# 96 token slots per expert and pass instead of 128 in a float32 mixture-of-experts kernel on one core

## The reference

```python
D_MODEL = 1024; SEQ = 256; D_FF = 3584; N_EXPERTS = 8; TOP_K = 2

def moe_ffn(h, router, w_gate_up, w_down):
    t = h.reshape(B * S, D)
    logits = (t @ router).astype(jnp.float32)
    top_v, top_i = lax.top_k(logits, TOP_K)
    gates = jax.nn.softmax(top_v, axis=-1)
    combine = jnp.sum(jax.nn.one_hot(top_i, N_EXPERTS) * gates[..., None], axis=1)
    out = jnp.zeros_like(t)
    for e in range(N_EXPERTS):
        out = out + combine[:, e:e + 1] * swiglu(t, w_gate_up[e], w_down[e])
    return out.reshape(B, S, D)

def swiglu(h, w_gate_up, w_down):
    g, u = jnp.split(h @ w_gate_up, 2, axis=-1)
    return (jax.nn.silu(g) * u) @ w_down
```

## Time and profile before

| what | value |
|---|---|
| median of 3 runs | 1673.5 us (1673.34 to 1674.12) |
| the profiled execution | 1673.83 us |
| its span, first to last instruction | 1672.0 us |
| mean granted TensorE clock | 0.968 |
| busy: PE, PEld, DVE, ACT | 94%, 74%, 66%, 54% |
| expert layer | from about 632 us to the end |
| HBM | 430 MB, 257 GB/s over the span |

### The profile page before, as it was taken

The page is one execution under the profiler, slowest core; times in us unless marked ns, Lnnn a source line. Parts: engine busy times, 40 slices in busy tenths (PEclk is TensorE's granted clock), DMA queues, the critical chain, the costliest instruction groups (busy, mean ns, idle before and its releaser), DMA issues.

```text
span 1672.0 us, 19744 instructions
## 1 busy us (share of the span) xinstructions
PE 1575.3 (94%) x6953; PEld 1245.3 (74%) x6953; DVE 1099.0 (66%) x834; ACT 898.7 (54%) x791; POOL 26.5 (2%) x77
## 2 busy tenths in 40 slices
PE   7997899999988788999999999999999999999997
PEld 4666478888755656887887888788788788788786
DVE  2103244545424335989889889889889888888885
ACT  2202144444225214767767667667667667667674
POOL 1100000000011000000000000000000000000000
PEclk9997899999988888999999999999999999999999
DMA  6341255555232043999999999999999999999992
GB/s 216 113 168 59 77 200 186 191 183 169 94 131 101 0 151 130 396 346 363 338 341 361 326 341 360 341 350 352 337 364 338 324 368 330 344 365 336 336 370 102
DMA packets 207394, 430.50 MB, mean 257 GB/s; under 512 B 13878, under 2 KB 52859, under 8 KB 207356
## 3 DMA queue, kind: packets, MB, share of 16 engines
q1 hardware_dynamic: 207356, 430.01, 72.1%
HBM read 428.91 MB, written 1.05 MB: 257 GB/s over the span
## 4 chain that ended last, share of the span: by engine, by line
PE 91%; DVE 4%; ACT 3%; issue 1%; DMA 1%; POOL 0%; SPq 0%; DVEq 0%; ACTq 0%; POOLq 0%
PE PS L1231 18%; PE PS L1232 18%; PE PS L1235 18%; PE PS L888 7%; PE PS L1037 5%; PE PS L1039 5%; PE PS L1038 5%; PE PS L856 3%; PE PS L930 3%; PE PS L1200 2%; PE PS L967 2%; PE PS L1133 1%; PE PS L1211 1%; ACT whi L636 1%; DVE xlo L1411 1%
## 5 line engine op out<-in xcount | busy, mean ns | idle before, releaser
L1399 DVE TENSOR_TENSOR wlo<-ring,whi 128x2048 fp32r<-128x2048 f32 x334 | 762.7, 2291 | 140.7 <-ACT whi L636 139.8
L636 ACT ACTIVATE whi<-ring 128x2048 fp32r<-128x2048 f32 x334 | 639.6, 1918 | 263.5 <-PE PS L1235 263.5
L1231 PE MATMUL PS<-whi,xhi 128*128 128x512 f32 x896 | 355.4, 397 | 2.8 <-DVE xlo L1426 2.4
L1232 PE MATMUL PS<-whi,xlo 128*128 128x512 f32 x896 | 350.2, 391 | 0.0
L1235 PE MATMUL PS<-wlo,xhi 128*128 128x512 f32 x896 | 240.0, 390 | 0.2 <-DVE wlo L1399 0.2
L1231 PEld LDWEIGHTS PS<-whi,xhi 128*128 128x128 f32 x896 | 168.9, 188 | 37.0 <-DVE xlo L1426 2.6
L1235 PEld LDWEIGHTS PS<-wlo,xhi 128*128 128x128 f32 x896 | 168.2, 188 | 36.2 <-DVE wlo L1399 0.6
L1232 PEld LDWEIGHTS PS<-whi,xlo 128*128 128x128 f32 x896 | 169.0, 189 | 33.8
L1231 PE MATMUL PS<-whi,hhi 128*128 128x512 f32 x440 | 174.4, 396 | 0.0
L1232 PE MATMUL PS<-whi,hlo 128*128 128x512 f32 x440 | 173.3, 394 | 0.0
L1367 DVE TENSOR_TENSOR wlo<-ring,whi 128x2048 fp32r<-128x2048 f32 x42 | 96.2, 2292 | 87.8 <-ACT whi L605 87.8
(11 more groups left out here) (255 smaller groups left out, 1413.1 us busy)
## 6 DMA issues: line engine op xcount, KB each, us to landing
ring<-in_moe_w_gate_up SPq DMA_DIRECT2D x448, 512.0 KB, 5.1
ring<-in_moe_w_down SPq DMA_DIRECT2D x224, 512.0 KB, 5.2
ring<-in_dense_w_gate_up SPq DMA_DIRECT2D x56, 512.0 KB, 4.6
ring<-in_dense_w_down SPq DMA_DIRECT2D x28, 512.0 KB, 4.3
ring<-in_a_w_in SPq DMA_DIRECT2D x6, 1536.0 KB, 6.6
ring<-in_mem_w_kv SPq DMA_DIRECT2D x2, 2048.0 KB, 10.4
ring<-in_a_w_out SPq DMA_DIRECT2D x2, 2048.0 KB, 7.8
ring<-in_b_w_out SPq DMA_DIRECT2D x2, 2048.0 KB, 7.9
```

The lines of the kernel that those rows point to most:

```text
L636: nc.scalar.activation(whi[:, j, :], ring[:, h * SLOT:(h + 1) * SLOT], ACT.Copy).then_inc(S("highs"), 1)
L1231: mm(out_, lhsT=xh, rhs=whi[:, j, c0:c0 + HD], start=first, stop=False)
L1232: mm(out_, lhsT=xl, rhs=whi[:, j, c0:c0 + HD], start=False, stop=False)
L1399: v.tensor_tensor(wlo[:, j, :], ring[:, h * SLOT:(h + 1) * SLOT], whi[:, j, :].bitcast(F32), ALU.subtract).then_inc(S("lows"), 1)
```

## The change

The slots per expert and pass go from 128 to 96. All that is derived from `CAP` follows: the width of the stationary operand, the partitions of the results, the moving columns of the gather, the tables, and `PASSES`, from 2 to 3. The count of passes compares the fullest expert with 96 and 192 in place of 128.

```diff
 CUTS = 3
-CAP = 128
+CAP = 96
 NEG = -float(2.0 ** 100)
```

## The result

The changed kernel takes 1682.65 us (median of 10 runs, 1675.77 to 1684.04) against 1673.2 us of the kernel before on the same occasions: ratio 1.0053, 95% interval 1.0042 to 1.0064. The forecast was 1671.0, and 1627 to 1678. The profiled execution of the changed kernel took 1684.04 us, its span 1682.2 us: 10.2 us more than the profiled one before. It is the slowest of the ten runs, and what follows splits up this one execution; by the medians the change costs 9.5 us.

What follows compares the result with a forecast made beforehand. The prediction took TensorE's matmuls to pace the expert loop. Its terms, -1.4 - 0.8 - 0.5 - 0.1 = -2.8 us, brought 1673.8 to 1671.0 us, with 8 in 10 from 1627 to 1678.

Steps and rivals of the forecast that it cites:

- Stationary 128 to 96: 0: Expert's fp32r products: the narrower load gains nothing, being hidden under the stream, except where a load stands bare.
- the fp32r excess of 10.8 ns: Expert's products: fp32r pace 226.7 ns against 215.9 for f32; if it belonged to the load, up to -43.5 us; taken as 0.
- rival (c): Expert's fp32r products run rougher at 96 columns: 5.8 ns more each, +23 us, 1694, or worse; chance 0.17.
- (a): Expert's fp32r products: the excess goes with the load's width, 2.7 ns a matmul, -10.9 us, 1660; chance 0.18.
- (b): Expert's fp32r products: the excess goes wholly once the stationary side isn't full, -43.5 us, 1628; chance 0.07.
- The turns of the hidden block load 128 columns still: 0: Transposes of the hidden block in each expert: their loads keep 128 columns, so no change in time.
- The gate matmuls: Four per expert, loading Sx, now 96 columns: 27 ns less each, -0.8 us in all.
- The first expert's split: -0.5 us: The split of x by ACT and DVE, bare before the first matmul, gets shorter: -0.22 - 0.27 = -0.5 us.
- The gather: 0: Gather of tokens, 32 matmuls in 3.57 us: already at the pace of its 128-column loads, so fewer moving columns give 0.
- The bare load behind a turn: -1.4 us: Second matmul after each of 56 turns of the hidden block: its unhidden load gets 25 ns shorter, -1.4 us.
- The clock: Expert loop: one or two more or fewer experts at 128.5 instead of 126.9 us, 1.6 us each, as luck.
- Routing, passes, transfers, y: 0: One more short DVE step in routing is covered, still one pass, transfers unchanged, the 2.8 us wait for y stays: 0.

Runs made afterwards that it cites:

- experiment 1: Changed kernel with its 96 slots, but each fp32r product of an expert loads all 128 columns: 1668.74 us, ratio 0.9978 to the kernel before.
- experiment 2: Kernel before with its 128 slots, but the fp32r products of an expert load 96 columns and write 96 partitions: 1689.3 us, ratio 1.0097.
- experiment 3: Kernel before, its expert products loading 127, 112, 64 or 32 columns: 1692.05, 1692.5, 1689.51 and 1694.0 us.
- experiments 5 to 7: ScalarE and VectorE split y four items earlier, in the kernel before, the changed kernel and the version of experiment 1: 1646.47, 1652.33 and 1641.32 us.

## Why the prediction was wrong, step by step

**The step that failed: "Stationary 128 to 96: 0".** The price of the narrow load was taken from f32 rows, where 4 and 96 columns give one pace, and the fp32r excess of 10.8 ns was put down as fixed or shrinking. Experiments 1 and 2 show a third thing, and experiment 3 shows it at every width tried below 128, a price for a load that isn't full: 226.7 to 230.0 ns, over a whole expert of the changed kernel 1.23 us, 9.8 us in all. That is rival (c) in its mild form, sized there at 5.8 ns and +23 us and given 0.17. f32 and fp32r matmuls do not answer alike to the width, and no row of fp32r had another width, so a price deserved as much weight as a gain. The range for 8 in 10 was widened downward for (a) and (b) alone. The f32 rows could have warned: with 256 moving columns f32 matmuls with full loads start (4.05 - 0.38)/17 = 215.9 ns apart in the kernel before, as those with 4 and 96 do, so they know neither the excess nor a gain or loss by the width, and could say nothing of fp32r.

```profile
56.67 4.05 PE L888 MATMUL PS<-ring,xT 128*128 128x256 f32 x18
```

The Trainium skill's page "TensorE: Matmul & The Clock Gate", section on weight-path perf modes, has a threshold in that very place: its fast weight load asks for 128 weights and a dtype that isn't FP32. The loss sets in at that threshold here (two thirds of the items at 127 columns lose the pace at fp32r, and 96 columns don't at f32), and I set it aside too lightly, since I looked for it in the duration of the load (188 against 190 ns) and not in the distance between matmuls. Whether it is the page's mechanism stays open, and the loads speak against it: they didn't get longer where the pace was lost, 187 to 188 ns at 127 columns and 162 at 96. Nor is it told why a third of the items keep 2.72 us at 127 columns.

**"The turns of the hidden block load 128 columns still: 0."** Wrong, it was a gain. The four transposes of a turn in the kernel before, just ahead of the earlier trace rows, and in the changed one:

```profile
999.36 0.60 PE L856 MATMUL PS<-ident,arena 128*128 128x128 f32 x4
```

```profile
1000.87 0.49 PE L856 MATMUL PS<-ident,arena 96*128 96x96 f32 x4
```

From there to the first product, which starts at 999.71 and at 1001.14, it is 0.35 us before and 0.27 after: 0.08 us less in each of 56 turns, 4.3 us in all. The prediction took the load of 128 columns for the bound, as in the gather, whose loads have the same width. But a transpose's load lasts 139 to 141 ns, not the gather's 192, and its matmuls start 108 ns apart with 128 moving columns, 83 with 96 and 70 with 80, though the load is as wide each time: the moving columns bind. This is most of the 0.61 us an expert that experiment 1 measures, 4.9 us in all. The gate matmuls were forecast at -0.8 us; their 32 loads fell from 191 to 164 ns, which agrees.

**The first expert's split: -0.5 us** was right: in the chain that ended last ScalarE's part went from 1.03 to 0.82 us and VectorE's from 1.23 to 0.97.

**The gather: 0** was right: 32 matmuls in 3.54 us, with 96 moving columns, against 3.57 in the earlier trace rows.

```profile
1635.73 3.54 PE PS L1200 x32
```

**The bare load behind a turn: -1.4 us** was right in size in the changed kernel, 0.29 us to the second matmul against 0.32 in the earlier trace rows:

```profile
1001.14 0.45 PE L1231 MATMUL PS<-whi,xhi 128*96 128x512 f32 x1
...
1001.43 0.39 PE L1232 MATMUL PS<-whi,xlo 128*96 128x512 f32 x1
...
1002.35 0.39 PE L1232 MATMUL PS<-whi,xlo 128*96 128x512 f32 x1
```

It needs both the narrow load and the narrow turn: in experiments 1 and 2, which have one each, the distance is 0.31 to 0.32 us. The next four start (1002.35 - 1001.43)/4 = 230.0 ns apart. This gain is already in the 1.23 us an expert above.

**The clock.** The forecast allowed a step or two of 1.6 us. It was three (four of six experts and one more behind the last cut, where there were two of six), 4.7 us. That the stretches go with the wait for y is shown by experiments 5 to 7, where the wait was taken away and the stretches went with it; that which experts are hit depends on the exact length of an expert is argued from experiment 2 (all six) and not shown by itself. The ten runs of the changed kernel are spread over 8 us, those of the kernel before over 3; that a changing number of stretches makes the spread is likely, but only one run of each has a profile.

**Routing, passes, transfers, y: 0** were right. The added step stands in DVE's timeline, where the cast now starts 0.38 us behind L1721 and not 0.19, and the product for the gather still waits for PE, 1.68 us:

```profile
626.57 0.15 DVE L1721 TENSOR_SCALAR arena<-arena 128x1 f32<-128x1 f32 x1
626.75 0.16 DVE L1723 SCALAR_TENSOR_TENSOR arena<-arena 128x1 f32<-128x1 f32 x1
626.95 0.15 DVE L1725 CAST cnt_i<-arena 128x1 int32<-128x1 f32 x1
...
629.21 2.47 DVE L1732 SCALAR_TENSOR_TENSOR xn<-xres,rx,PS 128x1024 f32<-128x1024 f32 x2 [1.68 <-PE PS L1218]
```

**The sum.** Narrow load +9.8, all else of the slots -4.9, clock +4.7, together +9.6 against 10.2 us measured between the profiled executions. The missing 0.6 us agree with what the last stretch has left over, where the clock is lower too (0.94 against 0.98). Against the forecast of 1671.0 the profiled execution is 13.0 us too long: 11.2 by the narrow load (+9.8 for -1.4), less 3.5 by all else of the slots (-4.9 for -1.4), and the remaining 5.3 by the clock and the end, which the forecast had called luck.

## What to carry to other kernels

In a dense stream of fp32r matmuls with 512 moving columns, keep the stationary side at its full 128 columns even when the data fill fewer: the load was hidden before, so narrowing it could not win, and it cost about 1.5% of each undisturbed matmul. Narrow what moves where the moving columns bind (the transposes here, not the gather), and count what a wait on TensorE costs in clock as well as in itself. When a term is multiplied by thousands, "no row shows it" is a reason to widen both ends, and to look for the effect in the distance between starts, not in durations.

## What the runs showed of the hardware

With fp32r and 512 moving columns at the full clock, undisturbed matmuls start 226.7 ns apart with 128 stationary columns, 230 with 96 or 64 and 232 with 32, though the loads are shorter; with 127 and 112 columns items of two paces mix, 226.7 and 233 ns, and 229 and 233. f32 matmuls with 256 moving columns start 216 ns apart with 4, 96 and 128 stationary columns alike. Stationary chunks at steps of 384 bytes cost about 1 ns more than at 512. f32 transposes of 128 stationary columns start 108, 83 and 70 ns apart with 128, 96 and 80 moving columns. Taking away a wait of 2.8 us on TensorE per expert (19.7 us) gained 26.4 us: an undisturbed expert is shorter by 126.89 - 123.83 = 3.06 us and not 2.8, 1.7 us more over seven waits; two half-clock stretches in the loop went with the wait (3.2 us); the rest, under 2 us, is not put down to anything.
